# Memory attention loop: output row and probability copies moved ahead of the newest tile's maximum and exponentials

## The reference

```python
def mem_attend(h, mem_kv, w_mem_q_l, w_mem_o_l):
    q = heads(h @ w_mem_q_l, MEM_HEADS, HEAD_DIM)            # 4 heads of 64
    s = jnp.einsum('bqhd,bkhd->bhqk', q, mem_kv[:, :, 0]) * ATTN_SCALE
    p = jax.nn.softmax(s, axis=-1)                           # over 256 memory tokens
    o = jnp.einsum('bhqk,bkhd->bqhd', p, mem_kv[:, :, 1])
    return o.reshape(..., MEM_W) @ w_mem_o_l
```

## Time and profile before

| | us |
|---|---|
| median of three executions | 2355.4 |
| the profiled execution | 2356.12 |
| its span (first to last instruction) | 2354.3 |
| loop, first logits to the end of the last row (about L2713 to L2634) | 1427.1 to 1506.9 |
| sample values L2758 | 1508.63 to 1522.47 |
| TensorE busy in the span | 2142.2 |
| VectorE busy | 1174.1 |
| ScalarE busy | 620.3 |

### The profile page before, as it was taken

How to read it: one execution, slowest core, us unless ns; L and a number is a source line. 1 busy time by engine, 2 the same in 40 slices (tenths; PEclk the granted TensorE clock), 3 DMA queues, 4 the chain that set the end, 5 groups by cost and what they waited for, 6 DMA issues and landing times. The chain is left out here.

```text
span 2354.3 us, 32990 instructions
## 1 busy us (share of the span) xinstructions
PE 2142.2 (91%) x12535; PEld 1973.5 (84%) x12535; DVE 1174.1 (50%) x2287; ACT 620.3 (26%) x1247; POOL 518.6 (22%) x569
## 2 busy tenths in 40 slices
PE   6999899999998966896789987889999999999997
PEld 5878788999998854553489976789999999999997
DVE  5059999998701315543154232254444444444445
ACT  5243222121112742342222233252111111111112
POOL 5776656778800002100000200030000000000000
PEclk9999999999987967997889985599999999999999
DMA  4022232367632438853074011021111101121001
GB/s 154 24 83 75 69 93 78 102 201 240 190 116 95 129 104 237 254 183 95 3 217 122 28 40 51 19 72 55 54 54 37 54 27 46 54 55 43 30 10 74
DMA packets 201025, 215.90 MB, mean 92 GB/s; under 512 B 47958, under 2 KB 186230, under 8 KB 200358
## 3 DMA queue, kind: packets, MB, share of 16 engines
q1 hardware_dynamic: 173206, 156.56, 22.6%
q10 hardware_dynamic: 26624, 29.87, 3.6%
q0 software_dynamic: 1040, 27.33, 3.4%
HBM read 178.94 MB, written 62.10 MB: 102 GB/s over the span
## 5 line engine op out<-in xcount | busy, mean ns | idle before, releaser
L3044 PE MATMUL p_g<-n_t_hi,g_hi 128*128 128x352 f32 x1056 | 342.7, 325 | 10.7 <-DVE g_lo L2936 7.8
L3044 PE MATMUL p_g<-n_t_lo,g_hi 128*128 128x352 f32 x1056 | 342.1, 324 | 0.0
L3044 PE MATMUL p_g<-n_t_hi,g_lo 128*128 128x352 f32 x1056 | 341.9, 324 | 0.0
L935 PE MATMUL pz<-w_hi,n_hi 128*128 128x384 f32 (+2 forms) x720 | 247.1, 343 | 0.6 <-issue 0.4
L935 PE MATMUL pz<-w_hi,n_lo 128*128 128x384 f32 (+2 forms) x720 | 240.8, 334 | 0.0
L935 PE MATMUL pz<-w_lo,n_hi 128*128 128x384 f32 (+2 forms) x720 | 240.7, 334 | 0.0
L3044 PEld LDWEIGHTS p_g<-n_t_hi,g_hi 128*128 128x128 f32 x1056 | 199.6, 189 | 11.9 <-issue 10.4
L843 DVE MATCH_REPLACE8 sel<-m,sel 128x1024 f32<-128x1024 f32 (+4 forms) x224 | 205.5, 923 | 0.0
L3044 PEld LDWEIGHTS p_g<-n_t_lo,g_hi 128*128 128x128 f32 x1056 | 199.6, 189 | 0.0
L3044 PEld LDWEIGHTS p_g<-n_t_hi,g_lo 128*128 128x128 f32 x1056 | 199.6, 189 | 0.0
L840 DVE MAX8 m<-sel 128x8 f32<-128x1024 f32 (+4 forms) x224 | 197.8, 927 | 0.2
(11 more groups left out here) (408 smaller groups left out, 4339.2 us busy)
## 6 DMA issues: line engine op xcount, KB each, us to landing
w_raw<-in_w_in SPq DMA_DIRECT2D x26, 768.0 KB, 4.7
relu<-z_qb SPq DMA_DIRECT2D x24, 512.0 KB, 4.8
w_first<-in_w_ffn_in SPq DMA_DIRECT2D x22, 512.0 KB, 6.5
g_raw<-in_w_ffn_in SPq DMA_DIRECT2D x22, 512.0 KB, 4.6
o_raw<-in_w_ffn_out SPq DMA_DIRECT2D x22, 512.0 KB, 4.5
z_b<-z ACTq DMA_DIRECT2D x48, 192.0 KB, 1.9
gates<-z ACTq DMA_DIRECT2D x48, 176.0 KB, 2.2
gate<-gates SPq DMA_DIRECT2D x24, 352.0 KB, 3.9
```

Of the source, the lines that this page charges most:

```text
L935: m = pe.matmul(out, tokens(a, k, i), b[:, n % 2, k, 0:w], start=(k == 0 and p == 0), stop=(k == KC - 1 and p == 2))
L3044: m = pe.matmul(p_g[:, t, e, 0:THIRD], a[:, u, e, w], b[:, k, t * THIRD:(t + 1) * THIRD], start=(k == 0 and p == 0), stop=(k == KC - 1 and ...
```

## The change

On VectorE, a turn began with the maximum of the newest tile (`it`), followed by the copy (`it - 2`), the output row (`it - 3`) and `om_lo` (`it - 3`). Now it begins with the output row, then comes the copy, then the maximum with its scaling, and `om_lo` stays last. On ScalarE, a turn began with the exponentials (`it - 1`), followed by the copy (`it - 2`) and `om_hi` (`it - 3`). Now the copy comes first, then the exponentials; `om_hi` stays last. No instruction and no wait is added or taken away, and nothing changes on TensorE, GpSimd or SyncE.

```diff
                 for it in range(LAST):                      # ScalarE
+                    i = it - 2
+                    if 0 <= i < NT:
+                        act.wait_ge(s_pt, i + 1)
+                        if i >= 2:
+                            act.wait_ge(s_pv, i - 1)
+                        act.activation(probs_t[:, i % 2, 0:512], p_t[:, 0, :], ACT.Copy).then_inc(s_ptA, 1)
                     i = it - 1
...
-                    i = it - 2
-                    if 0 <= i < NT:
-                        act.wait_ge(s_pt, i + 1)
-                        if i >= 2:
-                            act.wait_ge(s_pv, i - 1)
-                        act.activation(probs_t[:, i % 2, 0:512], p_t[:, 0, :], ACT.Copy).then_inc(s_ptA, 1)
...
                 for it in range(LAST):                      # VectorE
-                    i = it
-                    if i < NT:
-                        dve.wait_ge(s_qk, i + 1)
...
-                    i = it - 2
-                    if 0 <= i < NT:
-                        dve.wait_ge(s_pt, i + 1)
...
                     i = it - 3
                     if 0 <= i < NT:
                         dve.wait_ge(s_pv, i + 1)
...
                                           den[:, i % 4, :].unsqueeze(2).broadcast_to([P, BH, HD]), ALU.mult).then_inc(s_row, 1)
+                    i = it - 2
+                    if 0 <= i < NT:
+                        dve.wait_ge(s_pt, i + 1)
+                        if i >= 2:
+                            dve.wait_ge(s_pv, i - 1)
+                        dve.tensor_copy(probs_t[:, i % 2, 512:1024], p_t[:, 1, :]).then_inc(s_ptD, 1)
+                    i = it
+                    if i < NT:
+                        dve.wait_ge(s_qk, i + 1)
+                        if i >= 2:
+                            dve.wait_ge(s_exp, i - 1)
...
+                    i = it - 3
+                    if 0 <= i < NT:
                         dve.wait_ge(s_ohi, i + 1)
```

More of the change, by code:

```diff
@@ L2607, in _ @@
                 for it in range(LAST):
+                    i = it - 3
+                    if 0 <= i < NT:
+                        dve.wait_ge(s_pv, i + 1)
+                        dve.reciprocal(den[:, i % 4, :], den[:, i % 4, :]).then_inc(s_rd, 1)
+                        dve.wait_ge(s_rd, i + 1)
+                        if i >= 2:
+                            dve.wait_ge(s_ot, i - 1)
+                        dve.tensor_tensor(om_row[:, i % 2, :].rearrange("p (h e) -> p h e", h=BH), p_o[:, 0:256].rearrange("p (h e) -> p h e", h=BH),
+                                          den[:, i % 4, :].unsqueeze(2).broadcast_to([P, BH, HD]), ALU.mult).then_inc(s_row, 1)
+                    i = it - 2
[4 more added lines that the diff above has]
+                        dve.tensor_copy(probs_t[:, i % 2, 512:1024], p_t[:, 1, :]).then_inc(s_ptD, 1)
                     i = it
@@ L2617, in _ @@
                         dve.tensor_scalar(top[:, i % 2, :], rden[:, i % 2, :], -ATT_SCALE, None, ALU.mult).then_inc(s_nm, 1)
-                    i = it - 2
-                    if 0 <= i < NT:
-                        dve.wait_ge(s_pt, i + 1)
-                        if i >= 2:
-                            dve.wait_ge(s_pv, i - 1)
-                        dve.tensor_copy(probs_t[:, i % 2, 512:1024], p_t[:, 1, :]).then_inc(s_ptD, 1)
                     i = it - 3
                     if 0 <= i < NT:
[L2626 to L2632, removed]
                         dve.wait_ge(s_ohi, i + 1)
```

## The result

The changed kernel took 2328.64 us (median of four runs, 2323.26 to 2334.15) against 2356.82 us for the kernel before (four runs, 2354.61 to 2367.16): ratio 0.9893, 95% interval 0.9846 to 0.994. It is about 1% faster. The forecast was 2322 in a range of 2315 to 2342. Two more comparisons gave 0.9897 (0.9861 to 0.9934) and 0.9892 (0.9859 to 0.9926), with medians of 2324.77 and 2324.43.

A forecast was written before the change was run, and what follows sets the result against it. A chain of waits, not a full engine, bounds the loop: VectorE's maximum delays the output row. Three stretches fall from 73.34 to 39.6 us, 33.7 less, taking the median 2355.4 to 2322 us, range 2315 to 2342.

The forecast's parts named there:

- The chain: Loop turn: output row waits behind VectorE's maximum, leaving TensorE idle 2.63 us of 10.38; row first removes this.
- The turn: Mid-loop at full clock: row plus copy 1.4, turn of probabilities 0.93, values 1.74, giving 4.1 us.
- low-clock rival: Whole loop: clock stays low, turns of 7.34 us, kernel 2340.5 us; chance 0.15.
- last rival: Loop gets slower: exponentials ready only in the turn needing them, serial 12.1 us a turn, kernel 2366; chance 0.02.
- The clock: TensorE in the loop: full clock, as in the window attention, with one lapse near 1438.
- third case: Loop: the clock never lapses, 35.2 us in sum, 38.1 less, kernel 2317.3 us; chance 0.12.
- three stretches: TensorE from tile 2's logits to tile 3's, to tile 7's, to first work behind the loop: 73.34 to 39.6 us.
- likeliest case: Loop at full clock with one lapse: 39.6 us in sum, kernel 2322, own range 2317 to 2327; chance 0.67.
- first stretch: Logits of tile 2 to logits of tile 3: from 7.74 to 6.2 us, with the clock falling near 1437.9.
- ScalarE's part: ScalarE's copy ahead of exponentials: adds a serial 2.5 us, covered by 3.14 at full clock, leaving 0.64.
- Sizes behind the loop: Small products and output projection after the loop: no change counted, about 2 us to either side.

The follow-up runs named there:

- two half moves: Kernel before with VectorE reordered to row, maximum, copy, om_lo, or to copy, maximum, row, om_lo; ScalarE as before; loops of 69.3 and 65.8 us.
- e6_one_pause: Changed kernel with one extra VectorE reduction of 4224 columns ahead of tile 1's output row, stopping TensorE once in turn 4; loop 52.5 us.

## Why the prediction was right, and where it was not

**The chain.** Right. The wait for the output row was the pause of each turn, VectorE's maximum ahead of it was the cause, and the rest of TensorE's turn has no pause left. That row and copy both had to pass the maximum is shown by the two half moves.

**The turn.** Forecast 4.1 us, measured 4.21; VectorE's row and copy set it, as said. The warm logits were mis-sized (0.85, measured 1.07 from logits to turned row), which mattered only for the next step beyond the change. So were those at the low clock (1.71; 2.01 in `e6_one_pause`, 1448.48 to 1450.49), so a turn without pauses at 0.50 would be about 7.6 us, not 7.34, and the low-clock rival's time, as an estimate from these, about 2 us higher. The serial chain of the last rival adds up to 12.0 us, not 12.1, which changes nothing.

**The clock.** Forecast: full clock in the loop, with one lapse at its start. Three profiles of the change have it at 1.00 in the middle of the loop; two have the lapse and one has not. The first profile is therefore the forecast's third case (35.2 us for the three stretches, measured 5.33 + 16.86 + 14.04 = 36.2), and the other two are the likeliest case (39.6, measured in the third profile 7.79 + 18.10 and 14.29 to the loop's end, 40.2). The chance of 0.12 for no lapse was low, if one in three says anything, and its reason was wrong. The prediction laid the lapse to the pause of tile 1. In both lapsed profiles of the change the clock fell before that pause began: in the third one it was 1.00 until 1434.20 and 0.53 in the next 0.60 us, and the pause, 1.02 us before 1436.25, began at 1435.2:
```profile
1433.60:1434.20 0.60, 0.60 (x6) 0.49 (x6) 0.43 (x1) 0.43 (x1) 0.00 (x0) 1.00 0.00 0
1434.20:1434.80 0.60, 0.60 (x6) 0.30 (x2) 0.27 (x1) 0.60 (x4) 0.00 (x0) 0.53 0.00 0
...
1436.25 1.97 PE L2735 MATMUL p_t<-ident,probs 128*128 128x128 f32 x8 [1.02 <-ACT probs L2517]
```
The order copy, row, maximum has no such pause and lapsed twice. What all these profiles share is the pause of about 1.8 to 2.1 us ahead of tile 0's turn of the probabilities, but the profiles without a lapse have it too, so what decides stays open. The prediction also took the clock to be high from the loop's start; the first logits run at 0.50 in the trace of before (1427.00 to 1430.90), and the 0.99 of the earlier trace rows begins at 1431. That the clock "did not come back" with a pause of 2.68 in each turn held for the one profile that was read, and fails in another of the same kernel. The low-clock rival fell with every profile. The transposes did not hold the clock down: the unbroken middle stretch has 40 of them, ten a turn, in 137 instructions at 1.00. On this loop the rule of the Trainium skill ("TensorE: Matmul & The Clock Gate", Part 4) gave 2340.5 us and the trace disagrees with it.

**The first stretch.** Forecast 6.2 us, measured 5.33 without and 7.79 with the lapse; the turn of tile 1 came 2.58 us after the logits of tile 2, as forecast (2.6). With the lapse the clock fell near 1434, not near 1438, so the transposes of tile 1 and all its values were slow too. That the three stretches together came within 0.6 us of the forecast (40.2 for 39.6) is in part luck: the first was 1.6 longer, the others 0.4 and 0.6 shorter.

**ScalarE's part.** The price was right: in the turn above, copy and exponentials ran from 1444.13 to 1446.55, 2.42 us, and 0.70 were left to the turn of the probabilities at 1447.25. The pause at tile 1 was forecast at about 1.5 and is 1.45. What was not said is that this half of the edit brings nothing; the loop of 42.4 us without it and the ratio of 0.9994 with it alone say so.

**The size.** The three stretches were to lose 33.7 us; they lost 37.1 in the first pair of profiles and 33.2 where the lapse occurred (73.34 less 40.18). The mechanism and its price held. The median of 2328.64 lies inside the wide range only: the forecast with the lapse had 2317 to 2327, and the upper end of 2342 was there for the low-clock rival, which did not come. The medians moved less: by 28.2 us in the first comparison (2356.82 to 2328.64, 6.6 above the forecast), 29.2 and 24.3 in the two later ones. Two things lie between. One is the baseline: the profile showed a single loop of the kernel before, 79.9 us long, and the sum took it for every execution. One of three profiles has 62.5 us, which is 15.7 to 19.7 us longer than the loop of the changed kernel, and the two groups of times fit that, though only the profiled executions show their loops. That lowers the later baselines (medians 2354.0 and 2348.7), not the first, whose four runs all lie above 2354. In the last comparison the changed kernel's 2324.43 is 31 us below the middle of the long group (2355.2) and 14 below that of the short one (2338.6), so the gain depends on the clock that the kernel before happened to get. The other is the length of the phases ahead of the loop, which the sum held fixed: the loop starts between 1420.8 and 1432.8 us in the fourteen profiles, of kernels that are alike up to there. A large part of that spread arises between 490 and 742 us, where one stretch of the same work (first product of L941 to the last of L1072) took 239.8 to 248.9 us; why is not shown. How the 5 us that are short in the first comparison divide between these phases and the lapse stays open.

**Sizes behind the loop.** Counted as nothing, with 2 us to either side. The output projection was 32.8 to 35.6 us long and the feed-forward layer 796.0 to 798.1 in all profiles, against 33.9 and 796.2 in the first one. Each held to 2 us, but both can be long at once, by 3.7 us together in the profile with one pause. In the second and third profiles of the change the projection was 1.6 us longer than before.

## What to carry to other kernels

In a software pipeline on in-order engines, work whose inputs are already there goes ahead of work that waits for this turn's newest product, and all of what the next engine needs has to pass it, since half of the move mostly renames the wait. It need not be the oldest tile first: copy ahead of row was 0.17 us a turn shorter. When TensorE is at its low clock in a loop bound by a chain of waits, count a removed pause twice, once for itself and once for the clock, but only if little pause is left: with 1.60 or 2.07 us a turn left, the clock stayed at 0.50 for most of the loop. And take the baseline's clock from several profiles, since one and the same loop here took 79.9 us and 62.5.

## What the runs showed of the hardware

The granted clock made the same instructions of the same kernel take 10.38 us a turn in one execution and 6.78 in another, with pauses of 2.67 us in both. Fourteen products that nobody reads, put in that pause, gave a loop of 58.0 us where it had been 79.9 (62.5 in the execution in which the clock came back by itself), and made the whole kernel 0.6% faster. After one pause of 4.13 us the clock stayed at 0.50 for 10 us of unbroken work before it came back.
